# Attention scores of 256 columns as three fp32r passes instead of one fp32 matmul, with q and k split into high and low parts ahead of them

## The reference, cut to what matters

```python
q = q.reshape(bsz, t, heads, 128) * (128 ** -0.5)
k = k.reshape(bsz, t, heads, 128)
s = einsum('q e, k e -> q k', q, k).astype(float32)   # per head; causal, so of the 2 x 2 blocks of 128, three are needed
```

## Time and profile before

| what | value |
|---|---|
| median of 3 runs | 2127.61 us (2127.42 to 2128.24) |
| the profiled execution | 2127.44 us |
| its span in the profile | 2125.6 us |
| PE busy | 2114.7 us, 99% |
| DVE busy | 1474.8 us, 69% |
| ACT busy | 1029.1 us, 48% |

### The profile page before, as it was taken

The page is one execution under the profiler, slowest core; times in us unless marked ns, Lnnn a source line. Parts: engine busy times, 40 slices in busy tenths (PEclk is TensorE's granted clock), DMA queues, the critical chain, the costliest instruction groups (busy, mean ns, idle before and its releaser), DMA issues.

```text
span 2125.6 us, 25468 instructions
## 1 busy us (share of the span) xinstructions
PE 2114.7 (99%) x9470; PEld 1751.6 (82%) x9470; DVE 1474.8 (69%) x1902; ACT 1029.1 (48%) x1183; POOL 18.3 (1%) x24
## 2 busy tenths in 40 slices
PE   9999999999999999999999999999999999999998
PEld 7888888888888888888888888888888888888886
DVE  5797857864775775686778778577756856764875
ACT  6444445543543453454645554665434534544543
POOL 0000000000000000000000000000000000000000
PEclk9999999999999999999999999999999999999999
DMA  9655555656655656655555555456556566656553
GB/s 321 208 177 167 192 197 160 204 193 195 198 194 187 186 205 214 183 197 198 174 183 178 178 172 204 160 159 217 195 187 193 180 212 181 198 196 217 179 200 117
DMA packets 204077, 406.81 MB, mean 191 GB/s; under 512 B 6544, under 2 KB 9936, under 8 KB 203472
## 3 DMA queue, kind: packets, MB, share of 16 engines
q1 hardware_dynamic: 203856, 405.50, 58.0%
q10 hardware_dynamic: 128, 0.03, 0.0%
HBM read 403.41 MB, written 2.10 MB: 191 GB/s over the span
## 4 chain that ended last, share of the span: by engine, by line
PE 99%; DVE 1%; issue 0%; POOL 0%; ACT 0%; POOLq 0%; DVEq 0%
PE ps L1161 98%; PE ps L1304 1%; DVE x_sb L755 0%; PE ps L1388 0%; DVE tmp L1044 0%; POOL rst L351 0%; ACT tmp L483 0%; PE ps L1509 0%; DVE w_lo L711 0%; POOLq L104 0%; DVE act_pair L1081 0%; DVE act_pair L761 0%; DVE y_sb L1051 0%; DVEq L104 0%; DVE w_lo L789 0%
## 5 line engine op out<-in xcount | busy, mean ns | idle before, releaser
L711 DVE TENSOR_TENSOR w_lo<-w_raw,w_hi 128x1024 fp32r<-128x1024 f32 x750 | 910.4, 1225 | 573.2 <-ACT w_hi L381 570.1
L381 ACT ACTIVATE w_hi<-w_raw 128x1024 fp32r<-128x1024 f32 x750 | 789.0, 1060 | 898.2 <-PE ps L1161 894.1
L1161 PE MATMUL ps<-w_hi,act_pair 128*128 128x512 f32 x3456 | 1072.5, 390 | 0.7 <-DVE act_pair L1081 0.6
L1161 PEld LDWEIGHTS ps<-w_hi,act_pair 128*128 128x128 f32 x3456 | 647.2, 188 | 136.8 <-issue 2.2
L1161 PE MATMUL ps<-w_lo,act_pair 128*128 128x512 f32 x1728 | 670.3, 390 | 0.0
L1161 PE MATMUL ps<-w_hi,hid_hi 128*128 128x512 f32 x1280 | 498.8, 390 | 0.0
L1161 PE MATMUL ps<-w_hi,hid_lo 128*128 128x512 f32 x1280 | 498.1, 389 | 0.0
L1161 PE MATMUL ps<-w_lo,hid_hi 128*128 128x512 f32 x1280 | 498.0, 389 | 0.0
L1161 PEld LDWEIGHTS ps<-w_lo,act_pair 128*128 128x128 f32 x1728 | 324.1, 188 | 66.3 <-DVE w_lo L789 0.3
L818 DVE STREAM_TRANSPOSE qT<-kT 32x256 f32<-32x256 f32 x608 | 265.0, 436 | 42.0 <-ACT kT L593 32.7
L1161 PEld LDWEIGHTS ps<-w_lo,hid_hi 128*128 128x128 f32 x1280 | 240.3, 188 | 49.7
(11 more groups left out here) (104 smaller groups left out, 460.0 us busy)
## 6 DMA issues: line engine op xcount, KB each, us to landing
w_raw<-in_ffn_w_dram SPq DMA_DIRECT2D x256, 1024.0 KB, 5.3
w_raw<-in_sb_w_in_dram SPq DMA_DIRECT2D x48, 1024.0 KB, 5.1
w_raw<-in_ab_w_in_dram SPq DMA_DIRECT2D x36, 1024.0 KB, 5.1
w_raw<-in_ab_w_out_dram SPq DMA_DIRECT2D x16, 1024.0 KB, 5.0
w_raw<-in_sb_w_out_dram SPq DMA_DIRECT2D x16, 1024.0 KB, 5.0
w_raw<-in_ab_w_in_dram SPq DMA_DIRECT2D x6, 512.0 KB, 8.8
x_sb<-in_x_dram SPq DMA_DIRECT2D x8, 256.0 KB, 7.4
gpost<-in_norm_post_mix_dram SPq DMA_DIRECT2D x2, 1024.0 KB, 7.5
```

What stands on the lines that cost most here:

```text
L381: nc.scalar.activation(w_hi[:, t % RING, :, :], w_raw[:, t // 2, h:h + 2, :], ACT.Copy).then_inc(hi_ready, 1)
L711: nc.vector.tensor_tensor(w_lo[:, t % RING, :, :], w_raw[:, t // 2, h:h + 2, :], w_hi[:, t % RING, :, :].bitcast(F32), ALU.subtract).then_ ...
L1161: return nc.tensor.matmul(dst, lhsT, rhs, start=start, stop=stop, skip_group_check=True)
```

## The change

Four new views name memory that is idle while the scores are made: wide_hi and wide_lo (four heads by 256, in tiles 12 to 15 of hid_hi and hid_lo) and half_hi and half_lo (four heads by 128, in soft_hi and soft_lo). The operand of 256 columns goes into the wide pair, that of 128 into the half pair: in layer 0 k is wide and the second half of q is half, in layer 1 q is wide and the first half of k is half. ACT copies q's part to fp32r at tick 16 and k's at tick 21; DVE subtracts to get the low parts, q's at tick 22 and k's at tick 23. PE waits for both low parts in front of the group's scores, and makes each product of 256 columns as three fp32r passes. The products of 128 columns stay as they are.

```diff
+        wide_hi, wide_lo = (t[:, KT - HG:KT, :] for t in (hid_hi, hid_lo))
+        half_hi, half_lo = (t[:, :, :].rearrange("p c n -> p (c n)")[:, 0:HG * P].rearrange("p (h t) -> p h t", t=P)
+                            for t in (soft_hi, soft_lo))
...
# ACT
+            def split_high(dst, src, turned, done, grp):
+                act.wait_ge(turned, grp + 1)
+                nc.scalar.activation(dst, src, ACT.Copy).then_inc(done, 1)
+
-            def qkv_group(u, extras):
+            def qkv_group(u, extras, grp):
+                q, k = (qT[:, :, P:T], kT[:, :, :]) if grp < 2 else (qT[:, :, :], kT[:, :, 0:P])
+                q_hi, k_hi = (half_hi, wide_hi) if grp < 2 else (wide_hi, half_hi)
+                extras = {**extras, 16: [lambda: split_high(q_hi, q, s_q_turned, s_q_hi, grp)],
+                          21: [lambda: split_high(k_hi, k, s_turned, s_k_hi, grp)]}
...
# DVE
+            def split_low(dst, src, high, ready, done, grp):
+                dve.wait_ge(ready, grp + 1)
+                nc.vector.tensor_tensor(dst, src, high.bitcast(F32), ALU.subtract).then_inc(done, 1)
...
-                extras = merged(extras, turns(q_plan, qT, q_tok), k_turns,
+                q_turns = turns(q_plan, qT, q_tok)
+                last = max(q_plan)
+                q_turns[last] = [lambda: turn(qT, q_tok, range(16 - q_plan[last], 16)).then_inc(s_q_turned, 1)]
+                extras = merged(extras, q_turns, k_turns,
+                                {22: [lambda: split_low(q_lo, q, q_hi, s_q_hi, s_q_lo, grp)],
+                                 23: [lambda: split_low(k_lo, k, k_hi, s_k_hi, s_k_lo, grp)]},
                                 {24: [lambda h=h: scores(h) for h in range(HG)]})
...
# PE
+            def three(dst, still, moving):
+
+                mm(dst, still[0], moving[0], True, False)
+                mm(dst, still[0], moving[1], False, False)
+                return mm(dst, still[1], moving[0], False, True)
+
             def l0_scores(grp):
 
                 pe.wait_ge(s_turned, grp + 1)
+                pe.wait_ge(s_q_lo, grp + 1)
+                pe.wait_ge(s_k_lo, grp + 1)
...
                     mm(ps[:, 4 + h, 0:P], qT[:, h, 0:P], kT[:, h, 0:P], True, True)
-                    mm(ps[:, 4 + h, P:TRI], qT[:, h, P:T], kT[:, h, :], True, True).then_inc(s_sc, 1)
+                    three(ps[:, 4 + h, P:TRI], (half_hi[:, h, :], half_lo[:, h, :]), (wide_hi[:, h, :], wide_lo[:, h, :])
+                          ).then_inc(s_sc, 1)
...
             def l1_scores(grp):
 
                 pe.wait_ge(s_turned, grp + 3)
+                pe.wait_ge(s_q_lo, grp + 3)
+                pe.wait_ge(s_k_lo, grp + 3)
                 pe.wait_ge(s_olo, 2 * grp + 4)
                 for h in range(HG):
-                    mm(ps[:, 4 + h, 0:T], kT[:, h, 0:P], qT[:, h, :], True, True)
+                    three(ps[:, 4 + h, 0:T], (half_hi[:, h, :], half_lo[:, h, :]), (wide_hi[:, h, :], wide_lo[:, h, :]))
                     mm(ps[:, 4 + h, T:TRI], kT[:, h, P:T], qT[:, h, P:T], True, True).then_inc(s_sc, 1)
```

More of the change, by code:

```diff
@@ L213, in trunk_kernel @@
         s_turned = sem("s_turned")
+        s_q_turned = sem("s_q_turned")
+        s_q_hi = sem("s_q_hi")
+        s_k_hi = sem("s_k_hi")
+        s_q_lo = sem("s_q_lo")
+        s_k_lo = sem("s_k_lo")
         s_sc = sem("s_sc")
@@ L679, in _ @@
                 unit(2 + j, lambda j=j: gelu_u(j))
-            qkv_group(4, {t: [lambda m=m: gate_hi(m)] for m, t in enumerate(GATE_HI)})
-            qkv_group(7, l0_extras(0))
+            qkv_group(4, {t: [lambda m=m: gate_hi(m)] for m, t in enumerate(GATE_HI)}, 0)
+            qkv_group(7, l0_extras(0), 1)
             out_phase(U_OUT0, l0_extras(1), 1)
@@ L688, in suffix_matrices @@
                 nc.scalar.activation(sum_mats[:, :], cst[:, P:3 * P], ACT.Copy).then_inc(s_sums, 1)
-            qkv_group(U_IN1, {9: [suffix_matrices]})
+            qkv_group(U_IN1, {9: [suffix_matrices]}, 2)
             for g in range(1, L1_GROUPS):
-                qkv_group(U_IN1 + 3 * g, l1_extras(g - 1))
+                qkv_group(U_IN1 + 3 * g, l1_extras(g - 1), 2 + g)
             out_phase(U_OUT1, l1_extras(L1_GROUPS - 1), 3)
@@ L944, in l1_extras, with qkv_group @@
                         15: [lambda: o_lo(2 * grp + 4, 0, 4 * grp), lambda: o_lo(2 * grp + 5, 1, 4 * grp + 2)]}
-            def qkv_group(u, extras, q_plan, scores):
+            def split_low(dst, src, high, ready, done, grp):
+                dve.wait_ge(ready, grp + 1)
+                nc.vector.tensor_tensor(dst, src, high.bitcast(F32), ALU.subtract).then_inc(done, 1)
+            def qkv_group(u, extras, q_plan, scores, grp):
                 def scaled(i, dst, factor=None):
@@ L958, in qkv_group @@
                 k_turns[20] = [lambda: turn(kT, k_tok, range(12, 16)).then_inc(s_turned, 1)]
-                extras = merged(extras, turns(q_plan, qT, q_tok), k_turns,
+                q, k = (qT[:, :, P:T], kT[:, :, :]) if grp < 2 else (qT[:, :, :], kT[:, :, 0:P])
+                (q_hi, q_lo), (k_hi, k_lo) = (((half_hi, half_lo), (wide_hi, wide_lo)) if grp < 2 else
+                                              ((wide_hi, wide_lo), (half_hi, half_lo)))
+                q_turns = turns(q_plan, qT, q_tok)
[4 more added lines that the diff above has]
+                                 23: [lambda: split_low(k_lo, k, k_hi, s_k_hi, s_k_lo, grp)]},
                                 {24: [lambda h=h: scores(h) for h in range(HG)]})
@@ L1143, in _ @@
                            {t: [lambda m=m: gate_lo(m)] for m, t in enumerate(GATE_LO)})
-            qkv_group(4, merged(turns_u(1), gates), TURNS_GATE, lambda h: l0_scores(h, h))
-            qkv_group(7, l0_extras(0), TURNS_L0, lambda h: l0_scores(h, 4 + h))
+            qkv_group(4, merged(turns_u(1), gates), TURNS_GATE, lambda h: l0_scores(h, h), 0)
+            qkv_group(7, l0_extras(0), TURNS_L0, lambda h: l0_scores(h, 4 + h), 1)
             out_phase(U_OUT0, l0_extras(1), 1)
@@ L1150, in _ @@
             dve.wait_ge(s_pow, POWERS_TO_X[2])
-            qkv_group(U_IN1, {}, TURNS_L0, lambda h: l1_scores(h, 0))
+            qkv_group(U_IN1, {}, TURNS_L0, lambda h: l1_scores(h, 0), 2)
             for g in range(1, L1_GROUPS):
-                qkv_group(U_IN1 + 3 * g, l1_extras(g - 1), TURNS_L1, lambda h, g=g: l1_scores(h, g))
+                qkv_group(U_IN1 + 3 * g, l1_extras(g - 1), TURNS_L1, lambda h, g=g: l1_scores(h, g), 2 + g)
             out_phase(U_OUT1, l1_extras(L1_GROUPS - 1), 3)
```

## The result

The changed kernel takes 2132.25 us (median of 12 runs, 2131.98 to 2133.59) against 2127.57 for the kernel before (12 runs on the same chip, 2127.31 to 2128.92). That is 4.68 us more. The ratio is 1.0022 with a 95% interval of 1.0013 to 1.0031, so the kernel is slower, by about the 0.2% at which the prediction drew its line.

A forecast was written before the change was run, and what follows sets the result against it. PE was taken to bound the kernel, so waits add and savings subtract: +5.8 us of waits - 1.7 saved = +4.1 on the median 2127.61, giving 2131.7 us. The range was 2129.6 to 2133.7, the forecast case's own 2130.7 to 2132.7.

The forecast's parts named there:

- What bounds the kernel: PE, busy 2114.7 of 2125.6 us: work taken off its stream comes off the time, waits put in are added.
- The saving: 256-column scores: three fp32r passes instead of one fp32 product save 0.07 a head, 1.7 us over 24 heads.
- The rule of the Trainium skill: Weight loads overlap matmuls only for another row group; three loads would be paid, an estimated loss of about 0.7, time 2134.1.
- The place of k's low part: In DVE's list behind conversion 22, starting 1.14 after it; PE's scores 0.69 late in layer 1, 1.84 and 1.23 in layer 0.
- The release: From DVE's end of k's low part to PE's first score: 0.23 us taken, between 0.17 and 0.28.
- the difference of the waits: PE's waits before the six groups of scores were forecast at 1.84 + 1.23 + 2.76 = 5.83 us.
- My upper bound of 6.1: Sum of PE's waits before the scores if the release takes 0.28; 5.5 if it takes 0.17.
- that the splits would be in time: Rival: k's low part ends before PE reaches the scores, so no wait and 2125.9 us; chance 6%.
- The push on conversion 22: Rival: q's low part delays this DVE step in layer 1 too, 2 us more, 2133.7; 7% shared with the clock's fall.
- The clock: Rival: it falls after PE's new idle stretches; 7% shared with the push on conversion 22, at 2133.7 us.
- The line at 0.2%: Difference of 4.26 us (2131.87) that a measurement can about tell from no change; the forecast lay just inside it.
- the even chances: Probabilities given for the whole kernel's outcome: faster 0.02, same 0.49, slower 0.49.

The follow-up runs named there:

- experiment 1: Changed kernel with the 256-column scores as one plain fp32 matmul each again, its splits and waits kept: 2135.09 us, ratio 1.0034.
- experiment 3: Changed kernel with DVE's low parts one tick earlier, q's at 21 and k's at 22, ahead of conversion 22: 2126.07 us, ratio 0.9992.
- experiment 4: Changed kernel with q's low part moved to tick 23, in front of k's, both behind conversion 22: 2137.53 us, ratio 1.0047.
- experiment 7: Changed kernel with low parts at ticks 21 and 22, 128-column products first, one wait for k's low part: 2125.94 us, ratio 0.9990.
- experiment 8: experiment 3 with layer 1's 128-column products also as three fp32r passes, from the wrong keys: 2127.72 us, ratio 0.9999.
- experiment 5: Changed kernel with PE's waits for the turns and q's low part removed, only that for k's low part kept: 2131.29 us, ratio 1.0018.
- experiment 2: Changed kernel with its splits, but plain fp32 scores and no PE wait for the split parts: 2127.60 us, ratio 1.0000.
- experiment 6: Changed kernel with PE making a group's four 128-column products ahead of its waits for the low parts: 2127.14 us, ratio 0.9996.

## Why the prediction was right, step by step

The forecast was 4.1 us slower than before and 2131.7 us; measured are 4.7 and 2132.25. The mechanism was right, with its place and nearly all its distances.

- **What bounds the kernel:** right. Experiments 1, 3 and 4 move 2 to 6 us in and out of PE's stream, and each comes out whole in the time (in experiment 1 on the lower level).
- **The saving:** 1.7 forecast. Measured by experiments 3 and 7 it is 1.8 (0.30 or 0.29 a group), and 1.9 where the scores follow a wait. The passes of 256 columns are 0.12 apart, as the suffix sums showed. The rule of the Trainium skill that the prediction set against it ("TensorE: Matmul & The Clock Gate", "The mechanism") does not hold here: with it experiment 3 would have been slower than before. The same section also lets a load be pulled ahead when it goes to the background weight buffer, which the prediction left out. Its estimate by the rule was mis-summed too: 24 heads times that page's 107 ns, less 1.7, is an estimated loss of 0.9, not 0.7. Experiment 8 shows where hiding stops paying: loads still run under matmuls there, but a pass of 128 columns costs the 0.11 of the loads' spacing.
- **The place of k's low part:** right. It starts 1.14 or 1.15 behind conversion 22, which did not move against PE in layer 1 and in layer 0's second group, and slipped by 0.64 in layer 0's first, where 0.61 was forecast. The row for that one:

```profile
167.09 1.22 DVE L727 TENSOR_TENSOR w_lo<-w_raw,w_hi 128x1024 fp32r<-128x1024 f32 x1
168.22 1.22 DVE L964 TENSOR_TENSOR hid_lo<-kT,hid_hi 128x1024 fp32r<-128x1024 f32 x1
```

- **The release: the term that was mis-sized.** I took 0.23 from DVE's end to the first score's place, between 0.17 with no semaphore instruction behind the release and 0.28 with two. It is 0.33 (1107.69 to 1108.02). Two such instructions do start behind it, and they cost 0.16 together (experiment 5), not the 0.10 that twice 51 ns makes: they start 0.11 apart. Six times 0.10 is 0.6 us, and that is the difference of the waits, 6.5 against 5.8. My upper bound of 6.1 for this term was too low for the same reason.
- **The rest of the difference:** waits 0.65 more and saving 0.2 more leave 0.5 over the forecast's 4.1, which is the 4.59 in the groups.
- **The rivals:** that the splits would be in time did not come true in the changed kernel; experiment 3 makes it true, at 2126.07 where 2125.9 had been worked out for it. The push on conversion 22 did not come: q's low part leaves it its place. The clock stayed at full. Splits and waits did not disturb anything else (experiment 2).
- **The line at 0.2%:** the ratio's interval reaches from 0.13% to 0.31%. Whether the change is past 0.2% is as open as the even chances said.

## What to carry to other kernels

On an engine that runs a list in order, the place of a new instruction matters more than the engine's idle share: put what another engine waits for ahead of the next instruction that itself waits, not behind it. Here one tick in DVE's list was 6.2 us, and the same change turned from 4.7 us slower to 1.5 faster. Where it can't be moved, let the waiting engine first do what needs no new data; and count what its sequencer still has to do after the release.

## What was not expected of the hardware

- What PE's sequencer does behind the release has a price that its recorded 51 ns does not show. From DVE's end to the first weight load it is 0.05 to 0.08 us with no semaphore instruction started behind the release (experiment 5), 0.11 with one (experiment 6, layer 0) and 0.22 with two (the changed kernel), though the second of the two is for semaphores long raised.
- Three fp32r passes beat one fp32 matmul at 256 columns (0.35 against 0.435) and lose at 128 (0.33 against 0.22), since a pass of 128 columns comes to 0.11, almost as much as one of 256 (experiment 8).
- The upper level of the runs comes from the first ten microseconds. The profiles of experiments 2 and 7 are of that level (2128.85 and 2127.18). Where the kernel before shows the first two fp32r matmuls of 512 columns in 0.73, the profile of experiment 7 has them in 1.22:

```profile
6.25 0.73 PE L1161 MATMUL ps<-w_hi,act_pair 128*128 128x512 f32 x2 [0.61 <-DVE act_pair L1081]
```

```profile
6.42 1.22 PE L1189 MATMUL ps<-w_hi,act_pair 128*128 128x512 f32 x2 [0.20 <-DVE act_pair L1109]
```

  The view of windows gives a granted clock of 1.00 for this stretch in both, but for experiments 2 and 7 that is no measurement: the trace's record of the clock at its full level (2.4 GHz) begins only 4.9 us into the span in the kernel before, and 10.4 and 10.5 us into it in experiments 2 and 7 (4.9 to 6.4 in the other eight profiles). Until then matmuls of 512 columns start 0.42 to 0.43 apart in these two (7.44, 7.87, 8.29), about twice the 0.23 of later ones, which fits the lower level (1.2 GHz). So the clock came up 4 to 6 us later than in the others, though PE's list of work up to there is the same. The differences within the groups, all beyond 160 us, are free of this. What decides when it comes up is not shown.
